# A two-block transformer kernel: products ahead of modulation pieces in the first stage

## What is computed

```
mod   = silu(c) @ w_mod + b_mod            # 6 parts of 1024: shift, scale, gate, ...
mod_c = silu(c_ctx) @ w_mod + b_mod
hc = rmsnorm(ctx, norm1_g) * (1 + csc1) + csh1
kv_c = hc @ w_in[:, 1024:1536]             # keys and values of the context
hx = rmsnorm(x, norm1_g) * (1 + sc1) + sh1
q_x, k_x, v_x, ... = split(hx @ w_in)      # k and v use the same columns of w_in
```

## Time and profile before

| | |
|---|---|
| median of 3 runs | 1957.14 us (1951.63 to 1957.41) |
| profiled execution | 1954.66 us |
| its span, first to last instruction | 1952.8 us |
| mean granted TensorE clock | 0.975 |
| TensorE busy | 1844.9 us (94%) |
| VectorE, ScalarE, GpSimd busy | 983.0, 654.9, 85.1 us |
| HBM traffic | 181 GB/s over the span |

### The profile page before, as it was taken

One profiled execution on the slowest core, in us unless ns is written; L12 is line 12 of the kernel. 1 busy time (PEld: TensorE's weight loads), 2 busy tenths in 40 slices (PEclk: granted clock), 3 DMA queues, 4 the chain that ended last, 5 costly groups with the idle time before them and its releaser, 6 DMA issues.

```text
span 1952.8 us, 22760 instructions
## 1 busy us (share of the span) xinstructions
PE 1844.9 (94%) x9397; PEld 1336.6 (68%) x9403; DVE 983.0 (50%) x1620; ACT 654.9 (34%) x1126; POOL 85.1 (4%) x70
## 2 busy tenths in 40 slices
PE   5999999999999699999999899998998899999998
PEld 4877887788878434343443278897777788888886
DVE  4887887833542322231322153638384556536643
ACT  4455554432232301020110053424555333213233
POOL 0200001000000000000000000003030200000000
PEclk9999999999999699999999999999999999999999
DMA  9342423452351499999999942272121422233221
GB/s 323 127 130 77 141 76 98 130 173 87 103 231 68 167 415 421 421 422 421 420 421 422 409 141 81 70 220 65 44 84 38 156 71 85 89 119 105 73 89 43
DMA packets 174521, 355.10 MB, mean 182 GB/s; under 512 B 7154, under 2 KB 144466, under 8 KB 149074
## 3 DMA queue, kind: packets, MB, share of 16 engines
q1 hardware_dynamic: 170672, 338.85, 47.1%
q10 hardware_dynamic: 3458, 14.50, 2.1%
q0 software_dynamic: 288, 0.30, 0.1%
HBM read 345.53 MB, written 8.39 MB: 181 GB/s over the span
## 4 chain that ended last, share of the span: by engine, by line
PE 80%; DVE 9%; DMA 4%; ACT 4%; issue 2%; POOL 1%; SPq 0%; ACTq 0%; DVEq 0%
PE ps L492 77%; PE ps L495 3%; DMA rx<-in_w_exp_down 1%; DMA rx<-in_w_exp_up 1%; POOL X L2813 1%; DMA md<-in_w_mod 1%; DVE wsq1l L1896 1%; DVE wsp0l L1896 1%; DVE X L1905 1%; DVE small L2141 1%; ACT M L1250 1%; DVE k2l L1896 0%; ACT KR L1250 0%; DMA M2b<-m_spill 0%; DVE tb L1896 0%
## 5 line engine op out<-in xcount | busy, mean ns | idle before, releaser
L492 PE MATMUL ps<-H,wsq1h 128*128 128x512 f32 x640 | 200.4, 394 | 4.7 <-DVE wsq1l L1896 2.7
L492 PE MATMUL ps<-H,wsq0h 128*128 128x512 f32 x608 | 191.2, 396 | 0.2 <-DVE wsq0l L1896 0.2
L492 PE MATMUL ps<-rx,XE 128*64 128x512 f32 x752 | 178.5, 606 | 2.8 <-DMA rx<-in_w_exp_up 2.2
L492 PE MATMUL ps<-H,wsp1h 128*128 128x512 f32 x544 | 172.6, 399 | 1.4 <-DVE wsp1l L1896 1.4
L492 PEld LDWEIGHTS ps<-H,wsq1h 128*128 128x128 f32 x640 | 120.2, 190 | 30.6 <-issue 6.0
L492 PEld LDWEIGHTS ps<-H,wsq0h 128*128 128x128 f32 x608 | 114.5, 190 | 25.6 <-issue 2.3
L492 PE MATMUL ps<-H,wsq1l 128*128 128x512 f32 x320 | 125.3, 391 | 0.0
L492 PE MATMUL ps<-H,wsp0h 128*128 128x512 f32 x368 | 121.4, 408 | 2.1 <-ACT H L1250 2.1
L1896 DVE TENSOR_TENSOR wsq1l<-ring,wsq1h 128x1024 fp32r<-128x1024 f32 (+2 forms) x72 | 82.8, 1190 | 77.9 <-ACT wsq1h L1250 77.9
L492 PE MATMUL ps<-H,wsq0l 128*128 128x512 f32 x304 | 119.1, 392 | 0.0
L492 PEld LDWEIGHTS ps<-rx,XE 128*64 128x64 f32 x752 | 49.7, 138 | 95.9 <-issue 84.8
(11 more groups left out here) (378 smaller groups left out, 3458.6 us busy)
## 6 DMA issues: line engine op xcount, KB each, us to landing
rx<-in_w_exp_gate SPq DMA_DIRECT2D x49, 1024.0 KB, 17.2
rx<-in_w_exp_down SPq DMA_DIRECT2D x46, 1024.0 KB, 20.7
rx<-in_w_exp_up SPq DMA_DIRECT2D x45, 1024.0 KB, 19.1
ring<-in_w_in SPq DMA_DIRECT2D x37, 1024.0 KB, 5.5
ring<-in_w_up SPq DMA_DIRECT2D x20, 1024.0 KB, 5.2
ring<-in_w_exp_up SPq DMA_DIRECT2D x19, 1024.0 KB, 20.5
ring<-in_w_mod SPq DMA_DIRECT2D x18, 1024.0 KB, 7.3
ring<-in_w_exp_down SPq DMA_DIRECT2D x18, 1024.0 KB, 19.0
```

The costliest lines, as they stand in the source:

```text
L492: return pe.e.matmul(o, l, r, start=start, stop=stop, skip_group_check=True)
```

## The change

TensorE: the x spread comes before the first raw product, all context transposes, the turned vector `vec2` and the context spread too. Then pieces 0 and 1 in one go. In the loop a block's products come first, then the sum of the previous piece, then the raw product of the next. One block of values moves from behind q to ahead of keys(6). ScalarE writes the k slab's high part behind the context's copies, not ahead of them. VectorE handles two blocks in a row, then two pieces in a row.

```diff
@@ -677,22 +677,24 @@
                         i.then_inc(*S["pe_group"].tick(("cv" if name == "ctx" else "v", n)))
 
         to_t("x", xtok, 4, range(8))
-        mod_raw(0)
         norms("x", diag[:, 256:768])
-        to_t("ctx", ctok, 2, range(4))
-        mod_sum(0)
-        to_t("ctx", ctok, 2, range(4, 8))
-        mod_raw(1)
+        to_t("ctx", ctok, 2, range(8))
         turn_vec("vec2", vrow2[0:112, :], 112, [("v_turn", "vec2")], [("vec2_in", "vec2")])
         norms("ctx", diag[:, 0:256])
+        mod_raw(0)
+        mod_sum(0)
+        mod_raw(1)
         mod_sum(1)
-        for j, products, c in ((2, keys, 0), (3, keys, 1), (4, values_of, 0), (5, keys, 2), (6, keys, 3), (7, values_of, 1)):
+        for products, c, j in ((keys, 0, 2), (keys, 1, 3), (values_of, 0, 4), (values_of, 1, 5), (keys, 2, 6), (keys, 3, 7)):
+            products(c)
+            if j > 2:
+                mod_sum(j - 1)
             mod_raw(j)
-            products(c)
-            mod_sum(j)
+        values_of(2)
+        mod_sum(7)
         keys(4)
         keys(5)
-        values_of(2)
+        values_of(3)
         keys(6)
         keys(7)
         final["k"] = ("ck", 1)
@@ -701,7 +703,7 @@
         turn["banks"] = [6, 7]
         for _ in steps([("q", 0, 0)], Hh, Hl, T, lambda m: [("v_rope", (("q", 0, 0), "cos"))]):
             pass
-        for c in range(3, 8):
+        for c in range(4, 8):
             values_of(c)
         final["v"] = ("cv", 1)
         free[2], free[3], free[5] = [("v_take", ("v", 0))], [("v_take", ("v", 1))], [("v_take", "cv")]
@@ -1317,12 +1319,12 @@
             square(2 + i, f"x{i}_in", ("x", i), xtok[:, i, :], ("ss", 1 + i) if i else None)
         roots("x", 2, 4)
         take_t("x", Xv, T)
-        hi(slabs["k"])
         spread("x", tba, T)
         for i in range(2):
             square(i, f"ctx{i}_in", ("ctx", i), ctok[:, i, :], ("ss", i - 1) if i else ("ss", 5))
         roots("ctx", 0, 2)
         take_t("ctx", ctxT, L)
+        hi(slabs["k"])
         load("cst_in", "cst", cst[:, 0:C_ID], a["const_a"][:, 0:C_ID])
         spread("ctx", rsc, L)
 
@@ -1999,28 +2001,35 @@
         take_t("x", Xv, T, (1, 3))
         diagonals("x", 2, 4)
         take_t("x", Xv, T, (5, 7))
-        mod_row(0)
-        lo(slabs["k"])
         take_t("ctx", ctxT, L, (1, 3))
-        mod_out(0)
         diagonals("ctx", 0, 2)
         take_t("ctx", ctxT, L, (5, 7))
+        v.wait_ge(S["pe_turn"], "vec2")
+        cp(vt2[:, :], bank(where.get("vec2", 0), 0, 112)).then_inc(*S["v_turn"].tick("vec2"))
+        mod_row(0)
+        lo_half(slabs["k"])
+        mod_out(0)
+        lo_half(slabs["k"])
         mod_row(1)
         mod_out(1)
-        v.wait_ge(S["pe_turn"], "vec2")
-        cp(vt2[:, :], bank(where.get("vec2", 0), 0, 112)).then_inc(*S["v_turn"].tick("vec2"))
         for c in range(0, 8, 2):
-            for n in (c, c + 1):
-                norm_x(n)
-                norm_c(n)
-                if c < 6:
-                    mod_row(n + 2)
-                left_x(n)
-                left_c(n)
-                if c < 6:
-                    mod_out(n + 2)
-                if n == 1:
-                    lo(slabs["v"])
+            norm_x(c)
+            norm_c(c)
+            left_x(c)
+            norm_x(c + 1)
+            left_c(c)
+            norm_c(c + 1)
+            left_x(c + 1)
+            left_c(c + 1)
+            if c < 6:
+                mod_row(c + 2)
+                if c == 0:
+                    lo_half(slabs["v"])
+                mod_out(c + 2)
+                if c == 0:
+                    lo_half(slabs["v"])
+                mod_row(c + 3)
+                mod_out(c + 3)
 
 
 
```

## The result

The changed kernel takes 1964.37 us (median of 12 runs, 1957.05 to 1967.09), the kernel before 1953.68 us in 12 runs. The ratio is 1.005, with a 95% interval of 1.0036 to 1.0063: slower by 7 to 12 us. The forecast was +3.9 us, too little to be told from no change. The direction was right; the size was not.

The account below looks back on a forecast made before the run. TensorE, nearly full until 300 us, was taken to pass on any shift of the keys' rotation. Rotation +2.2 and clock +1.7 gave +3.9 us: 1958.6 or 1961.0 on two bases, middle 1959.8, range 1953.0 to 1965.5.

Parts of the forecast that it names:

- The yardstick: Start of the keys' rotation on VectorE, 66.91 us before; forecast 69.1, +2.2 us, passed on to the span's end.
- Up to the first block: Start through block 0's norm: first raw product at 21.6 us, first norm at 27.2 instead of 31.46, 4.3 won.
- the low patch at the very start: TensorE's half-clock stretch at the first raw product, 1.89 against 0.98 us; cost up to 0.9, counted as gone.
- The constants' transfer: Moves about 5 us earlier on ScalarE's queue; could delay piece 3 from 33.1 to 34.7 at most, hidden by v's low part.
- SyncE's queue gains: SyncE's transfer reissues wait for raw products 0 to 3, which were to come no later than before.
- The new waits: TensorE stands 2.6 us at sum(4) and again at sum(6) for VectorE's row copy; pair to pair 9.9 us.
- The clock: A new wait may drop TensorE's clock, costing 0, 1.7 or 3.4 us; one fall at 1.7 taken for both.
- my schedule: Timing without clock loss: norms of blocks 0, 2, 4, 6 at 27.2, 39.5, 49.4, 59.3 us, rotation 69.1, +2.2.
- Slower, by the clock: Rival, 18%: both new waits drop the clock for 3.4 us each, first raw at half level 0.9; +9.9, 1965.8 us.
- The waits don't arise: Rival, 12%: VectorE's pair short enough to keep TensorE full, 5.3 us of waits vanish; -3.1, 1952.8 us.
- nothing arrives: Rival, 10%: shift taken up between 67 and 113 us, or the edit's halves cancel; 1955.9 us.
- the forecast's own case: The main forecast, 60%: bounds from no fall (+2.2) to two short falls with late first raw (+6.5), 1956.9 to 1963.6 us.

Follow-up runs that it names:

- with the clock held: Changed kernel with useless products in all TensorE waits (start and loop) and constants issued late: 1954.09 us, ratio 1.0010 to the kernel before.
- the start alone: Kernel before with only the change's start (spread, context transposes, k's high part, constants' transfer moved), loop of before: 1954.39 us, ratio 1.001.
- with the transfer late: The change's start with the loop of before, constants' transfer issued behind block 3; also called "with the constants late": 1951.77 us, ratio 0.9989.
- its loop alone: Kernel before with only the change's loop (TensorE's order, VectorE's pairs), start of before: 1964.84 us, ratio 1.0066.
- its start filled: The change's start, loop of before, constants late, plus 12 useless products in TensorE's waits before the first keys: 1953.47 us, ratio 0.9986.
- two kernels with values(2) behind: values(2) moved behind keys(7) and first q slab: in the kernel before 1951.27 us, 0.9985; in the late-constants, filled-start kernel 1948.37 us, 0.9976.

## Why the prediction was right or wrong

**The yardstick** was right. The rotation is 11.08 us later and the span 11.1 longer; the busy times of the stages behind it are the same.

**Up to the first block.** The path that I laid (transposes, spread, squares, roots, first copy, blocks 6 and 7, first raw product) is the one in the profile. Its start was put at 21.6 and came at 22.86. Part of it is the execution: the x transposes took 4.91 us and ended 0.6 later. Part is the clock: the context spread took 1.09 instead of 0.61. The first norm was put at 27.2 and came at 29.68; with the clock held it was 27.55. The step that failed is the one on the low patch at the very start, "I have counted it gone": there were two such patches, and the second took in keys(0).

**The constants' transfer.** I bounded its harm at 1.6 us, on piece 3, hidden. It fell on piece 2: 13.4 us from issue to landing in the changed kernel, 14.6 in the start alone, 12.1 with the transfer late. In the changed kernel it landed at 31.2 and raw(2) came at 35.34 behind slow keys, so it cost nothing there. In the start alone it cost TensorE up to 2.3 us of waiting. The mechanism was named; the piece that it would fall on was wrong. I also wrote that SyncE's queue gains; it did not. The last piece was issued at 40.06 instead of 36.80 us, since the raw product that it waits for came later, but it was wanted only at 62.49, and that cost nothing.

**The new waits** were right: 2.39 and 2.42 for 2.6, and 9.93 us from pair to pair for 9.9.

**The clock** is the term that was mis-sized. I took one fall at 1.7 us for both waits and none at the start. Measured at the rotation: 77.99 - 69.64 = 8.4 us between the changed kernel and the one with all waits filled and the constants late. Its parts between these two are 3.9 before the norm of block 2 (43.78 and 39.91; 0.3 of it is the earlier end of the x transposes) and 3.0 and 1.5 in the two steps. Against my schedule they are 4.3, 3.0 and 1.6, together 8.9; that 2.2 + 8.9 gives the 11.1 measured is no check, since the parts were taken as what the schedule leaves over.

**The rule that I weighed too lightly.** I set the waits of the earlier trace rows, which left the clock alone, against the statement of the Trainium skill ("TensorE: Matmul & The Clock Gate", section "HAM oscillation") that waits between short bursts drop the clock each time. In the profiled executions of the changed kernel and of its loop alone, three of four waits of 2.4 us were followed by a fall, so "each time" is nearly right here, though the page's own waits are longer than these, about 3 to 5 us. The waits in the earlier trace rows were a poor witness against it. I gave their sum, 5.0 us, but each of them was short, the longest this one:

```profile
90.42 0.70 PE L492 MATMUL ps<-H,wsp1h 128*128 128x512 f32 x2 [1.38 <-DVE wsp1l L1896]
```

The single waits in the two late stretches of the earlier trace rows, in which the clock fell, were 1.73 and 2.62 us. The new waits were forecast at 2.6 us, near the longer of these and at its price of 3.4 us, and I priced the pair of them by the shorter.

**The rivals.** "Slower, by the clock" is what happened, by its mechanism. That its size nearly fits (+9.9 forecast, +10.7 in the medians) is partly luck: it had 6.8 us in the two steps, where 4.6 were lost, and 0.9 at the start, where up to 4.3 were. "The waits don't arise" and "nothing arrives" are out by the rows above. The chance of 18% was too low: I had counted the falls as unlikely to come together. That one cause, too little work on TensorE between waits, makes all of them is argued; what the runs show is that useless products in the waits kept the clock at 1.00 in each place.

**The numbers.** The measured 1964.37 lies inside the range, near its upper end, and that is in part luck: the forecast's own case ended at 1963.6 and at +6.5 us, and the difference was +10.7. The kernel before measured 1953.68 over 12 runs, lower than the three runs that I had, so the difference is larger than the absolute time suggests.

## What to carry to other kernels

In a hand-ordered queue, ask of each wait what is ready behind it. Here one sum queued ahead of a block's products cost 2.4 us twice; products ahead of it brought the step from 9.9 to 8.4 us.
When a change thins out TensorE's work, price the clock at every wait that it lengthens and at the work that follows, not as one accident for all: here, at the rotation, the order cost 2.7 us (69.64 against 66.91) and the clock 8.4.
Before paying for an earlier start, find the stage that sets the next hand-off; moving work ahead into an idle stretch moved the first norm by 1 to 4 us and brought nothing in the time that a pair of kernels could show.

## What I had not expected

Useless products made the kernel faster: with those in the loop's waits, at the start and the constants late it went from 1.005 to 1.0010, and these intervals do not meet; the 40 in the loop's waits alone gave 1.0028, whose interval overlaps the first.
A transfer of 545 KB issued 6 us earlier on another queue (22.68 in the start alone, 28.67 in before) delayed a transfer that was issued ahead of it: piece 2, issued at 18.31, landed at 32.9, while the constants, issued at 22.68, landed 6.5 us later, at 29.2.

```profile
cst<-in_const_a ACTq DMA_DIRECT2D x1, 545.0 KB, 6.5
```

The stretch from rotation to end differed between profiled executions of kernels that do the same work there: 1947.3 - 67.17 = 1880.1 us with the constants late and 1951.4 - 65.46 = 1885.9 with its start filled, or 1946.8 - 65.32 = 1881.5 and 1953.8 - 64.00 = 1889.8 us in two kernels with values(2) behind. No run here says why. One profile of each kernel can rank them wrongly; medians of 10 to 12 runs do better, and several of the comparisons above stay open even so.
